# An encoder layer on one core: attention's scores and value products in three passes of rounded halves and rests, in place of full fp32 matmuls

## The chip, the core and the metric

The kernel runs on one core of a Trainium2 chip. The metric is the device time of one execution in microseconds (us); of several runs, the median.

## What is computed

One layer of a bidirectional encoder over 512 tokens of width 2048. The part that the change touches is attention with 8 query heads, 2 key and value heads and head width 128:

```python
q = rms_norm(q.reshape(B, S, ATT_HEADS, HEAD_DIM), q_norm_w)
k = rms_norm(k.reshape(B, S, ATT_KV_HEADS, HEAD_DIM), k_norm_w)
q = apply_axial_rope(q, cos, sin) * (HEAD_DIM ** -0.5)
k = apply_axial_rope(k, cos, sin)
...
s = jnp.einsum('bqhgd,bkhd->bhgqk', q_blk, k).astype(jnp.float32)
p = jax.nn.softmax(s, axis=-1).astype(v.dtype)
return jnp.einsum('bhgqk,bkhd->bqhgd', p, v)
```

Around it stand a conditioning product (`mod`), an input projection `h @ w_in` whose other columns feed a gated linear recurrence (HGRN2, 8 heads), an output projection, and a feed-forward part (up projection, convolution of width 3, GeGLU, down projection). All is float32.

## The kernel before

Five instruction streams (TensorE, VectorE, ScalarE, GpSimd and SyncE with the DMA queue) are written out by hand and tied by semaphores. An engine executes its own stream in order, so what stands behind a waiting instruction waits too.

The large projections don't use fp32 matmuls. Each operand is kept as a half `hi` rounded to the type fp32r and a rest `lo` = value - `hi`. `three_passes` (L1285 to L1288) adds three fp32r matmuls of 128x128 by 128x512 into one PSUM bank: hi by lo, hi by hi, lo by hi. `split_hi` (ScalarE, L437) and `split_lo` (VectorE, L818) make the two parts of each block of weights. Attention's own products are single calls on fp32 tiles instead.

TensorE's stream through the attention stage is a chain of query tiles (`q_tile`). A tile has 16 steps `s`. Each step is one `three_passes` of the input projection (`project_step`), and the attention of the head before hangs between the steps. For head h, whose query tile was projected just before:

- After step 2, `rope_mm` (L1319, L1320): two fp32 matmuls, for the sum of squares and the rotated copy of the queries. Keys use it as well, as r = 0 and 1 (`kv_side`, within the first query tile); head h has r = h + 2.
- On ScalarE, `rope_front` copies the projected tile out of PSUM (L482, L483), which also frees what the PE needs for the next `rope_mm`, and it waits for `rope_done` of the r before. `rope_rs` (L487, L489) makes 1/rms with a logarithm and an exponential.
- On VectorE, `rope_back` (L893 to L900): four tensor operations of 128x512, the last of which writes the tile `QT` (or `KTT` for keys) and signals `rope_done`.
- After steps 7 to 10, `scores` (L1336): one fp32 matmul for each of four blocks of 128 queries, into a bank each. The first waits for `rope_done`.
- VectorE at steps 8 to 12: `att_max` (L904) for each block, and `att_scale` (L909, L911) one step behind; between them ScalarE's `att_exp` (L496).
- After steps 12 to 15, `turn_probs` (L1346): four transposes of a block of probabilities into bank 6 or 7 in turn. Block qt waits until the copy of block qt - 2 has left the bank.
- ScalarE at step 12 `vsa_copy` (L513, the values into `VSA`) and at steps 13 to 15 and step 1 of the next tile `pt_copy` (L503, bank into `PT`).
- After step 4 of the tile after next, `att_values` (L1355): four fp32 matmuls into bank 2; then ScalarE's `att_store` (L518).

VectorE makes its two `split_lo` of the next tile at steps 5 and 7, between `rope_back` and `att_max`. Head 7 has no query tile behind it; its attention hangs in the first recurrence head (`hg_head`), whose steps `g` carry on VectorE a `split_lo` at g = 4 and 12 and a `chunk_row` (L1033, L1036) at g = 6, 10 and 14.

```python
def turn_probs(h, qt):
    n = h * TT + qt
    pe.wait_ge(prob_ready, n + 1)
...
        pe.wait_ge(pt_ready, n - 1)
```

Of the kernel before, what the change touches and what calls it, by code (L numbers as in the profile page):

```python
# [27 lines left out]
F32 = mybir.dt.float32  # L28
# [79 lines left out]
def hybrid_encoder_layer(nc, x, c, w_ada, b_ada, norm_mix_pre, norm_mix_post, w_in, q_norm, k_norm,  # L108
# [44 lines left out]
    KTT = at("KTT", [P, KV_HEADS, S], F32, OV)  # L153
    V2 = at("V2", [P, KV_HEADS, S], F32, OV + 4 * KB)
    VSA = at("VSA", [P, TT, P], F32, OV + 8 * KB)
# [4 lines left out]
    QT = at("QT", [P, S], F32, OV + 20 * KB)  # L160
    PM = [at(f"PM{n}", [P, S], F32, OV + o * KB) for n, o in enumerate((22, 24, 18, 38))]
    PT = at("PT", [P, TT, S], F32, OV + 26 * KB)
# [42 lines left out]
    with ExitStack() as ctx:  # L205
# [26 lines left out]
        prob_turned, pt_ready, att_pv, att_out = sem("prob_turned"), sem("pt_ready"), sem("att_pv"), sem("att_out")  # L232

# [189 lines left out]
        def _(act):  # L423
# [75 lines left out]
            def pt_copy(h, qt):  # L499
                act.wait_ge(prob_turned, h * TT + qt + 1)  # L500
                if qt == 0 and not (isinstance(h, int) and h == 0):
                    act.wait_ge(att_pv, h)
                act.activation(PT[:, :, qt * P:(qt + 1) * P],  # L503
                               PB[6 + qt % 2][:, :].rearrange("p (k q) -> p k q", q=P), ACT.Copy).then_inc(pt_ready, 1)

            def vsa_copy(h, group):

                if isinstance(h, int) and h == 0:
                    act.wait_ge(v_ready, KV_HEADS)
                else:  # L510
                    act.wait_ge(att_pv, h)
                src = V2[:, group, :] if isinstance(group, int) else V2[:, bass.ds(group, 1), :]
                act.activation(VSA[:, :, :].rearrange("p a b -> p (a b)"), src, ACT.Copy).then_inc(vsa_ready, 1)  # L513
# [293 lines left out]
        def _(dve):  # L807
# [81 lines left out]
            def rope_back(r, dst):  # L889
# [6 lines left out]
                dve.wait_ge(rope_t, r * 2 + 1)  # L896
                dve.tensor_tensor(SQA[:, :], T1[:, :], SQA[:, :], ALU.add).then_inc(rope_t, 1)
                dve.wait_ge(rope_t, r * 2 + 2)
                dve.wait_ge(rope_rstd, r + 1)
                dve.tensor_tensor(dst, SQA[:, :], RSA[:, :], ALU.mult).then_inc(rope_done, 1)  # L900
# [12 lines left out]
            def att_side(h, s):  # L913
                if s == 2:
                    rope_back(h + KV_HEADS, QT[:, :])
# [5 lines left out]
            def q_tile(i, e, first):  # L921
                h = i * 2 + e
                for s in range(16):
                    if first and e == 0 and s in (3, 9):
                        rope_back(s // 9, KTT[:, s // 9, :])
                    if not (first and e == 0):
                        att_side(h - 1, s)
# [3 lines left out]
            q_tile(0, 0, True)  # L931
            q_tile(0, 1, True)
            with dve.Fori(1, ATT_HEADS // 2) as i:
                q_tile(i, 0, False)
                q_tile(i, 1, False)
# [109 lines left out]
            def hg_head(h, i, e, first):  # L1045
                for g in range(STEPS):
                    bank = ((g // 16) + e + 1) % 2
                    if first and e == 0:
                        if g < 16:
                            att_side(ATT_HEADS - 1, g)  # L1050
# [185 lines left out]
        def _(pe):  # L1236
# [93 lines left out]
            def scores(h, group, qt):  # L1330
# [4 lines left out]
                rhs = KTT[:, group, :] if isinstance(group, int) else KTT[:, bass.ds(group, 1), :]  # L1335
                pe.matmul(PB[SCORE_BANKS[qt]][:, :], QT[:, qt * P:(qt + 1) * P], rhs, start=True, stop=True).then_inc(score_done, 1)  # L1336

            def turn_probs(h, qt):
# [4 lines left out]
                else:  # L1343
                    pe.wait_ge(pt_ready, n - 1)
# [356 lines left out]
```

## Time and profile before

| what | value |
|---|---|
| median of 3 runs | 2675.48 us (2674.86 to 2677.21) |
| profiled execution: span of the trace | 2672.3 us |
| TensorE matmul busy | 2580.3 us, 97% |
| VectorE busy | 1293.3 us, 48% |
| ScalarE busy | 833.6 us, 31% |
| TensorE in the chain that ended last | 92% |
| attention stage, from the first key rope to the last value product | about 204 to 398 us of the span |

The span is that of the profiled execution, from its first to its last instruction; the run's own time holds some 3 us around it. A matmul's length in the trace holds the time that its data take through the array, so that matmuls overlap in it: for their pace one reads start to start. A weight load (PEld) runs beside the matmul before.

### The profile page before, as it was taken

What the parts mean: (1) busy time and instruction counts of PE and PEld (TensorE: products, weight loads), DVE (VectorE), ACT (ScalarE), POOL (GpSimd) and SP (SyncE); (2) the same over time, 40 slices, a digit from 0 to 9 for tenths busy, and PEclk for the clock granted to TensorE, in tenths of its full rate; (3) what the DMA queues carried; (4) which work ended last, traced back from release to release, by engine and by line L of the source; (5) the groups of instructions that cost most, each with busy time, mean ns of one, the idle gap of its engine ahead of it and who ended that gap; (6) DMA issues with size and microseconds to landing.
All of it is one profiled execution on the core that took longest, in us unless ns stands there. A gap on an engine that the chain in (4) does not pass through costs nothing.

```text
span 2672.3 us, 32532 instructions
## 1 busy us (share of the span) xinstructions
PE 2580.3 (97%) x11944; PEld 2077.9 (78%) x11944; DVE 1293.3 (48%) x1538; ACT 833.6 (31%) x1112; POOL 6.5 (0%) x16
## 2 busy tenths in 40 slices
PE   5889999999999998989999999999999999999998
PEld 3446668888888877877888888888888878888887
DVE  4774456667766655345333333333333333334334
ACT  5116652222222232234222222222222222323222
POOL 0000000000000000000000000000000000000000
PEclk9889999999999999999999999999999999999999
DMA  7872136555655542423333333333333333222422
GB/s 229 229 201 65 47 104 219 166 181 181 193 169 174 169 129 68 177 96 110 102 100 96 94 94 94 94 97 102 100 94 94 94 110 100 96 94 98 162 94 110
DMA packets 396373, 335.78 MB, mean 126 GB/s; under 512 B 9670, under 2 KB 354720, under 8 KB 394016
## 3 DMA queue, kind: packets, MB, share of 16 engines
q1 hardware_dynamic: 394816, 324.54, 39.9%
q0 software_dynamic: 1504, 10.50, 1.0%
q8 instruction: 37, 0.61, 0.1%
q14 instruction: 16, 0.13, 0.0%
HBM read 326.60 MB, written 8.40 MB: 125 GB/s over the span
## 4 chain that ended last, share of the span: by engine, by line
PE 92%; DMA 3%; DVE 3%; ACT 2%; SPq 1%; issue 1%; DVEq 0%; ACTq 0%
PE bank L1286 27%; PE bank L1288 26%; PE bank L1287 26%; DMA AS_raw<-in_w_ada_dram 3%; PE bank L1456 2%; PE bank L1454 2%; PE bank L1250 1%; PE bank L1489 1%; PE bank L1355 1%; PE bank L1336 1%; PE bank L1476 1%; PE bank L1519 1%; PE bank L1346 0%; DVE ACC L856 0%; SPq L316 0%
## 5 line engine op out<-in xcount | busy, mean ns | idle before, releaser
L1286 PE MATMUL bank<-H_lo,W_hi 128*128 128x512 f32 x2240 | 918.5, 410 | 1.7 <-ACT QW L483 1.4
L1288 PE MATMUL bank<-H_hi,W_lo 128*128 128x512 f32 x2240 | 875.3, 391 | 0.0
L1287 PE MATMUL bank<-H_hi,W_hi 128*128 128x512 f32 x2240 | 874.4, 390 | 0.0
L818 DVE TENSOR_TENSOR W_lo<-W_raw,W_hi 128x1024 fp32r<-128x1024 f32 x400 | 481.2, 1222 | 200.8 <-ACT W_hi L437 189.7
L1286 PEld LDWEIGHTS bank<-H_lo,W_hi 128*128 128x128 f32 x2240 | 421.8, 188 | 109.4 <-issue 30.0
L1287 PEld LDWEIGHTS bank<-H_hi,W_hi 128*128 128x128 f32 x2240 | 422.1, 188 | 94.8 <-issue 15.3
L1288 PEld LDWEIGHTS bank<-H_hi,W_lo 128*128 128x128 f32 x2240 | 421.3, 188 | 89.8
L437 ACT ACTIVATE W_hi<-W_raw 128x1024 fp32r<-128x1024 f32 x400 | 410.6, 1049 | 169.7 <-DMA W_raw<-in_w_in_dram 73.9
L1286 PE MATMUL bank<-W_lo,GS_hi 128*128 128x512 f32 x704 | 275.4, 391 | 4.7 <-DVE GS_lo L1190 4.7
L1287 PE MATMUL bank<-W_hi,GS_hi 128*128 128x512 f32 x704 | 275.1, 391 | 0.0
L1288 PE MATMUL bank<-W_hi,GS_lo 128*128 128x512 f32 x704 | 275.1, 391 | 0.0
L1190 DVE TENSOR_TENSOR GS_lo<-G,GS_hi 128x512 fp32r<-128x512 f32 x88 | 60.7, 692 | 266.7 <-ACT GS_hi L771 266.7
L1036 DVE SCALAR_TENSOR_TENSOR AB_acc<-AB_raw,SM,AB_acc 128x1024 f32<-128x1024 f32 x120 | 153.8, 1281 | 25.9 <-DMA AB_raw<-in_w_ada_dram 24.8
L1153 DVE SCALAR_TENSOR_TENSOR CA<-bank,VEC,CA 128x511 f32<-128x511 f32 x44 | 33.0, 750 | 264.4 <-ACT CA L734 264.4
L1286 PEld LDWEIGHTS bank<-W_lo,GS_hi 128*128 128x128 f32 x704 | 132.8, 189 | 32.9 <-issue 5.1
L1287 PEld LDWEIGHTS bank<-W_hi,GS_hi 128*128 128x128 f32 x704 | 132.8, 189 | 27.5
L1288 PEld LDWEIGHTS bank<-W_hi,GS_lo 128*128 128x128 f32 x704 | 132.7, 189 | 27.6
L771 ACT ACTIVATE GS_hi<-G 128x512 fp32r (+1 forms) x88 | 55.3, 631 | 303.2 <-PE bank L1288 300.8
L734 ACT ACTIVATE CA<-bank,VEC 128x512 f32<-128x512 f32 x44 | 34.3, 779 | 356.6 <-PE bank L1288 356.6
L1153 DVE SCALAR_TENSOR_TENSOR CB<-bank,VEC,CB 128x511 f32<-128x511 f32 x44 | 33.0, 750 | 231.6 <-ACT CB L734 231.6
L734 ACT ACTIVATE CB<-bank,VEC 128x512 f32<-128x512 f32 x44 | 34.3, 779 | 254.8 <-PE bank L1288 254.8
L1286 PE MATMUL bank<-W_lo,H_hi 128*128 128x512 f32 x256 | 102.9, 402 | 7.4 <-DVE H_lo L1073 3.8
(185 smaller groups left out, 2077.9 us busy)
## 6 DMA issues: line engine op xcount, KB each, us to landing
W_raw<-in_w_up_dram SPq DMA_DIRECT2D x176, 512.0 KB, 4.5
AB_raw<-in_w_ada_dram SPq DMA_DIRECT2D x128, 512.0 KB, 4.5
W_raw<-in_w_in_dram SPq DMA_DIRECT2D x104, 512.0 KB, 4.0
W_raw<-in_w_down_dram SPq DMA_DIRECT2D x88, 512.0 KB, 3.5
AS_raw<-in_w_ada_dram SPq DMA_DIRECT2D x32, 1024.0 KB, 8.9
W_raw<-in_w_out_dram SPq DMA_DIRECT2D x32, 512.0 KB, 3.7
XT<-in_x_dram SPq DMA_DIRECT2D x4, 1024.0 KB, 8.0
XR<-in_x_dram POOLq DMA_DIRECT2D x4, 1024.0 KB, 12.6
```

The lines of the kernel that those rows point to most:

```text
L437: act.activation(W_hi[:, k % SLOTS, :], W_raw[:, k % RAW, :], ACT.Copy).then_inc(hi_ready, 1)
L734: act.activation(dst, PB[2 * e + half][:, :], ACT.Identity, bias=col(VEC, jj + V_CONVB), scale=col(VEC, jj + V_CONVW[1])).then_inc((ca_rea ...
L771: act.activation(GS_hi[:, k % SLOTS, :], src, ACT.Copy).then_inc(gs_hi, 1)
L818: dve.tensor_tensor(W_lo[:, k % SLOTS, :], W_raw[:, k % RAW, :], W_hi[:, k % SLOTS, :].bitcast(F32), ALU.subtract).then_inc(lo_ready, 1)
L1036: ins = dve.scalar_tensor_tensor(AB_acc[:, :], AB_raw[:, kt % 2, :], col(SM, CS + kt), AB_acc[:, :], ALU.mult, ALU.add)
L1153: dve.scalar_tensor_tensor(buf[:, e, 1:S], bank[:, 0:S - 1], col(VEC, jj + V_CONVW[0]), buf[:, e, 1:S], ALU.mult, ALU.add).then_inc(conv_l, 1)
L1190: dve.tensor_tensor(GS_lo[:, k, :], src, GS_hi[:, k, :].bitcast(F32), ALU.subtract).then_inc(gs_lo, 1)
L1286: pe.matmul(acc, st_hi, mv_lo, start=start, stop=False)
L1287: pe.matmul(acc, st_hi, mv_hi, start=False, stop=False)
L1288: return pe.matmul(acc, st_lo, mv_hi, start=False, stop=stop)
L1454: pe.matmul(halves(bank[:, t])[:, :, 1, :], YY[:, 0, t], halves(XX[:, 0, t])[:, :, 1, :], start=True, stop=True)
L1456: ins = pe.matmul(halves(bank[:, t])[:, :, 0, :], XX[:, 1, t], halves(YY[:, 1, t])[:, :, 0, :], start=True, stop=True)
```

## The change

Scores and value products go through `three_passes`. So every operand of theirs gets a rounded half and a rest.

- `KTT`, `QT`, `PT`, `VSA` become `KT_hi`, `QT_hi`, `PT_hi`, `VSA_hi` of type fp32r, and four tiles `_lo` are added where the recurrence's outputs are kept later.
- `rope_back` has two more instructions for each of its 10 calls, a cast to `hi` and a subtraction for `lo`, each behind a semaphore of the one before. `rope_done` comes after the last.
- VectorE gets `vsa_lower` (one for each head, at step 13) and `pt_lower` (four for each head, at steps 13 to 15 and step 1 of the next tile), which reads the transposed block in PSUM and subtracts `PT_hi`.
- `turn_probs` and `att_values` wait for `pt_low` and `vsa_low`, the subtractions, where they waited for ScalarE's copies.

```diff
-                dve.tensor_tensor(dst, SQA[:, :], RSA[:, :], ALU.mult).then_inc(rope_done, 1)
+                dve.tensor_tensor(T1[:, :], SQA[:, :], RSA[:, :], ALU.mult).then_inc(rope_t, 1)
+                dve.wait_ge(rope_t, r * 3 + 3)
+                dve.tensor_copy(hi, T1[:, :]).then_inc(rope_hi, 1)
+                dve.wait_ge(rope_hi, r + 1)
+                dve.tensor_tensor(lo, T1[:, :], hi.bitcast(F32), ALU.subtract).then_inc(rope_done, 1)
...
+            def vsa_lower(h, group):
+                dve.wait_ge(vsa_ready, h + 1)
+                src = V2[:, group, :] if isinstance(group, int) else V2[:, bass.ds(group, 1), :]
+                dve.tensor_tensor(VSA_lo[:, :, :].rearrange("p a b -> p (a b)"), src,
+                                  VSA_hi[:, :, :].rearrange("p a b -> p (a b)").bitcast(F32), ALU.subtract).then_inc(vsa_low, 1)
+
+            def pt_lower(h, qt):
+                dve.wait_ge(pt_ready, h * TT + qt + 1)
+                q = slice(qt * P, (qt + 1) * P)
+                dve.tensor_tensor(PT_lo[:, :, q], PB[6 + qt % 2][:, :].rearrange("p (k q) -> p k q", q=P),
+                                  PT_hi[:, :, q].bitcast(F32), ALU.subtract).then_inc(pt_low, 1)
...
+                if s == 13:
+                    vsa_lower(h, group)
+                if s >= 13:
+                    pt_lower(h, s - 13)
+
+            def att_tail(h, s):
+                if s == 1:
+                    pt_lower(h, TT - 1)
...
-                rhs = KTT[:, group, :] if isinstance(group, int) else KTT[:, bass.ds(group, 1), :]
-                pe.matmul(PB[SCORE_BANKS[qt]][:, :], QT[:, qt * P:(qt + 1) * P], rhs, start=True, stop=True).then_inc(score_done, 1)
+                keys = [t[:, group, :] if isinstance(group, int) else t[:, bass.ds(group, 1), :] for t in (KT_hi, KT_lo)]
+                q = slice(qt * P, (qt + 1) * P)
+                three_passes(PB[SCORE_BANKS[qt]][:, :], QT_hi[:, q], QT_lo[:, q], *keys, True, True).then_inc(score_done, 1)
...
-                    pe.wait_ge(pt_ready, n - 1)
+                    pe.wait_ge(pt_low, n - 1)
...
-                pe.wait_ge(pt_ready, h * TT + TT)
-                pe.wait_ge(vsa_ready, h + 1)
+                pe.wait_ge(pt_low, h * TT + TT)
+                pe.wait_ge(vsa_low, h + 1)
                 for k in range(TT):
-                    ins = pe.matmul(PB[2][:, :], VSA[:, k, :], PT[:, k, :], start=(k == 0), stop=(k == TT - 1))
+                    ins = three_passes(PB[2][:, :], VSA_hi[:, k, :], VSA_lo[:, k, :], PT_hi[:, k, :], PT_lo[:, k, :],
+                                       k == 0, k == TT - 1)
```

Two places of the order show it. In the changed kernel the lines of `three_passes` are L1320 to L1322 and the rope's are L898 to L909.

TensorE, steps 8 and 9 of a query tile with the scores between them, before:

```order
L1336 MATMUL bank<-KTT,QT 128x512
L1294 REGISTER_ALU
L1286 MATMUL bank<-H_lo,W_hi 128x512 [waits lo_ready]
L1287 MATMUL bank<-H_hi,W_hi 128x512
L1288 MATMUL bank<-H_hi,W_lo 128x512
L1336 MATMUL bank<-KTT,QT 128x512
```

The same place now:

```order
L1320 MATMUL bank<-KT_lo,QT_hi 128x512
L1321 REGISTER_ALU
L1321 MATMUL bank<-KT_hi,QT_hi 128x512
L1322 MATMUL bank<-KT_hi,QT_lo 128x512
L1328 REGISTER_ALU
L1320 MATMUL bank<-H_lo,W_hi 128x512 [waits lo_ready]
L1321 MATMUL bank<-H_hi,W_hi 128x512
L1322 MATMUL bank<-H_hi,W_lo 128x512
```

Each fp32 score has become three passes; the steps between them are as they were.

VectorE, from the last scale of a head (the tile `PM_87`) to the rope of the next, before:

```order
L911 TENSOR_SCALAR PM_87<-PM_87,SM 128x512 [waits prob_rcp]
L890 REGISTER_ALU
L893 TENSOR_TENSOR T_82<-QW,COS 128x512 [waits rope_in]
L895 TENSOR_TENSOR SQA<-bank,SIN 128x512 [waits rope_psum]
L896 ISA
L897 TENSOR_TENSOR SQA<-T_82,SQA 128x512 [waits rope_t]
L898 REGISTER_ALU
L900 TENSOR_TENSOR QT<-SQA,RSA 128x512 [waits rope_rstd,rope_t]
```

Now, from behind that scale and a wait for `vsa_ready`:

```order
L925 TENSOR_TENSOR VSA_lo<-V_77,VSA_hi 128x512
L931 TENSOR_TENSOR PT_lo<-bank,PT_hi 128x4x128 [waits pt_ready] x4
L895 REGISTER_ALU
L898 TENSOR_TENSOR T_82<-QW,COS 128x512 [waits rope_in]
L900 TENSOR_TENSOR SQA<-bank,SIN 128x512 [waits rope_psum]
L901 ISA
L902 TENSOR_TENSOR SQA<-T_82,SQA 128x512 [waits rope_t]
L903 REGISTER_ALU
L905 TENSOR_TENSOR T_82<-SQA,RSA 128x512 [waits rope_rstd,rope_t]
L906 REGISTER_ALU
L907 CAST QT_hi<-T_82 128x512 [waits rope_t]
L909 TENSOR_TENSOR QT_lo<-T_82,QT_hi 128x512 [waits rope_hi]
```

Five subtractions stand where VectorE had nothing, and two instructions stand behind the rope's product.

## Rows read from the trace of the kernel before

**Rows 1.** The page: busy time of the engines; the chain by line.

```profile
PE 2580.3 (97%) x11944; PEld 2077.9 (78%) x11944; DVE 1293.3 (48%) x1538; ACT 833.6 (31%) x1112; POOL 6.5 (0%) x16
...
PE bank L1286 27%; PE bank L1288 26%; PE bank L1287 26%; DMA AS_raw<-in_w_ada_dram 3%; PE bank L1456 2%; PE bank L1454 2%; PE bank L1250 1%; PE bank L1489 1%; PE bank L1355 1%; PE bank L1336 1%; PE bank L1476 1%; PE bank L1519 1%; PE bank L1346 0%; DVE ACC L856 0%; SPq L316 0%
```

**Rows 2.** TensorE's waits from 200 to 400 us: us in total, times, longest.

```profile
PE bank L1286 <- ACT QW L483: 1.4, 1, 1.4
PE bank L1346 <- ACT PT L503: 0.8, 1, 0.8
PE bank L1319 <- ACT QW L483: 0.6, 1, 0.6
```

**Rows 3.** Groups by line and form: busy us, mean ns of one, idle before.

```profile
L1336 PE MATMUL bank<-KTT,QT 128*128 x48 | 24.5, 592 | 0.0
...
L895 DVE TENSOR_TENSOR SQA<-bank,SIN 128x512 f32<-128x512 f32 x10 | 6.9, 691 | 21.3 <-PE bank L1320 21.3
...
L1143 DVE CAST H_hi<-HT 128x512 fp32r<-128x512 f32 x8 | 3.4, 421 | 0.0
```

**Rows 4.** Timeline of TensorE, head 3: start us, us, instruction.

```profile
291.67 0.39 PE L1287 MATMUL bank<-H_hi,W_hi 128*128 128x512 f32 x1
...
293.05 0.39 PE L1287 MATMUL bank<-H_hi,W_hi 128*128 128x512 f32 x1
...
294.60 0.40 PE L1287 MATMUL bank<-H_hi,W_hi 128*128 128x512 f32 x1
...
299.27 0.40 PE L1287 MATMUL bank<-H_hi,W_hi 128*128 128x512 f32 x1
...
302.67 0.60 PE L1346 MATMUL bank<-ident,PM 128*128 128x128 f32 x4
```

**Rows 5.** Timeline of TensorE, steps of the first query tile.

```profile
220.35 0.39 PE L1286 MATMUL bank<-H_lo,W_hi 128*128 128x512 f32 x1
...
223.07 0.39 PE L1286 MATMUL bank<-H_lo,W_hi 128*128 128x512 f32 x1
```

**Rows 6.** Timelines of VectorE, then ScalarE, head 3.

```profile
289.54 0.69 DVE L900 TENSOR_TENSOR QT<-SQA,RSA 128x512 f32<-128x512 f32 x1 [1.31 <-ACT RSA L489]
...
299.23 0.69 DVE L904 TENSOR_REDUCE SM<-bank 128x1 f32<-128x512 f32 x1 [0.27 <-PE bank L1336]
...
300.77 0.16 DVE L909 RECIPROCAL SM<-SM 128x1 f32<-128x1 f32 x1 [0.26 <-ACT PM L496]
...
299.96 0.69 ACT L496 ACTIVATE PM<-bank,SM 128x512 f32<-128x512 f32 x1 [0.70 <-DVE SM L904]
...
301.16 0.59 ACT L503 ACTIVATE PT<-bank 128x512 f32<-128x512 f32 x1
```

**Rows 7.** Timelines of VectorE, then ScalarE, around the ropes of the keys.

```profile
212.19 0.69 DVE L900 TENSOR_TENSOR KTT<-SQA,RSA 128x512 f32<-128x512 f32 x1 [1.32 <-ACT RSA L489]
...
213.41 0.59 ACT L482 ACTIVATE SQA<-bank 128x512 f32<-128x512 f32 x1
```

**Rows 8.** Timeline of TensorE before and at head 0's first score.

```profile
228.69 0.39 PE L1288 MATMUL bank<-H_hi,W_lo 128*128 128x512 f32 x1
229.15 1.13 PE L1336 MATMUL bank<-KTT,QT 128*128 128x512 f32 x2
```

**Rows 9.** Timelines of VectorE, ScalarE and TensorE, head 7.

```profile
384.56 1.28 DVE L1036 SCALAR_TENSOR_TENSOR AB_acc<-AB_raw,SM,AB_acc 128x1024 f32<-128x1024 f32 x1
...
388.23 1.23 DVE L818 TENSOR_TENSOR W_lo<-W_raw,W_hi 128x1024 fp32r<-128x1024 f32 x1 [0.26 <-ACT W_hi L437]
...
386.48 0.69 ACT L496 ACTIVATE PM<-bank,SM 128x512 f32<-128x512 f32 x1 [1.61 <-DVE SM L904]
...
389.35 0.63 PE L1346 MATMUL bank<-ident,PM 128*128 128x128 f32 x4 [0.83 <-ACT PT L503]
```

**Rows 10.** TensorE's timeline at the down projection; window with granted clock (seventh value).

```profile
2181.39 0.76 PE L1286 MATMUL bank<-W_lo,GS_hi 128*128 128x512 f32 x1 [4.73 <-DVE GS_lo L1190]
...
2182.00:2186.00 4.00, 4.00 (x11) 3.12 (x10) 3.45 (x4) 2.02 (x3) 0.00 (x0) 0.50 0.21 61
```

More of the change, by code:

```diff
@@ L151, in hybrid_encoder_layer @@
     OV = WK + 24 * KB
-    KTT = at("KTT", [P, KV_HEADS, S], F32, OV)
+    KT_hi = at("KT_hi", [P, KV_HEADS, S], F32R, OV)
     V2 = at("V2", [P, KV_HEADS, S], F32, OV + 4 * KB)
-    VSA = at("VSA", [P, TT, P], F32, OV + 8 * KB)
+    VSA_hi = at("VSA_hi", [P, TT, P], F32R, OV + 8 * KB)
     QW = at("QW", [P, S], F32, OV + 10 * KB)
@@ L159, in hybrid_encoder_layer @@
     T1 = at("T1", [P, S], F32, OV + 16 * KB)
-    QT = at("QT", [P, S], F32, OV + 20 * KB)
+    QT_hi = at("QT_hi", [P, S], F32R, OV + 20 * KB)
     PM = [at(f"PM{n}", [P, S], F32, OV + o * KB) for n, o in enumerate((22, 24, 18, 38))]
-    PT = at("PT", [P, TT, S], F32, OV + 26 * KB)
+    PT_hi = at("PT_hi", [P, TT, S], F32R, OV + 26 * KB)
+    PT_lo = at("PT_lo", [P, TT, S], F32R, MXB + 16 * KB)
+    KT_lo = at("KT_lo", [P, KV_HEADS, S], F32R, MXB + 24 * KB)
+    VSA_lo = at("VSA_lo", [P, TT, P], F32R, MXB + 28 * KB)
+    QT_lo = at("QT_lo", [P, S], F32R, MXB + 30 * KB)
     COS = at("COS", [P, S], F32, OV + 34 * KB)
@@ L232, in hybrid_encoder_layer @@
         prob_turned, pt_ready, att_pv, att_out = sem("prob_turned"), sem("pt_ready"), sem("att_pv"), sem("att_out")
+        rope_hi, pt_low, vsa_low = sem("rope_hi"), sem("pt_low"), sem("vsa_low")
         sig_ready, stage_ready, vt_ready, vs_turned, vs_ready = (
@@ L502, in pt_copy @@
                     act.wait_ge(att_pv, h)
-                act.activation(PT[:, :, qt * P:(qt + 1) * P],
+                act.activation(PT_hi[:, :, qt * P:(qt + 1) * P],
                                PB[6 + qt % 2][:, :].rearrange("p (k q) -> p k q", q=P), ACT.Copy).then_inc(pt_ready, 1)
@@ L886, in _, with rope_back @@
             split_lo(0, 4, 9)
-            def rope_back(r, dst):
+            def rope_back(r, hi, lo):
                 dve.wait_ge(rope_in, r + 1)
@@ L919, in att_side, with q_tile @@
                     att_scale(h, s - 9)
-            def q_tile(i, e, first):
+                if s == 13:
[5 more added lines that the diff above has]
+                    pt_lower(h, TT - 1)
+            def q_tile(i, e, first, group):
                 h = i * 2 + e
@@ L924, in q_tile @@
                     if first and e == 0 and s in (3, 9):
-                        rope_back(s // 9, KTT[:, s // 9, :])
+                        rope_back(s // 9, KT_hi[:, s // 9, :], KT_lo[:, s // 9, :])
                     if not (first and e == 0):
-                        att_side(h - 1, s)
+                        att_side(h - 1, group, s)
+                    if not first:
+                        att_tail(h - 2, s)
                     if s - 1 in SPLIT_STEPS:
                         split_lo(i, 4, 2 * ATT_PROLOGUE + 2 * e + 2 + SPLIT_STEPS.index(s - 1))
-            q_tile(0, 0, True)
-            q_tile(0, 1, True)
+            q_tile(0, 0, True, 0)
+            q_tile(0, 1, True, 0)
             with dve.Fori(1, ATT_HEADS // 2) as i:
-                q_tile(i, 0, False)
-                q_tile(i, 1, False)
+                q_tile(i, 0, False, i // 3)
+                q_tile(i, 1, False, i // 2)
             def stage(h, j, bank):
@@ L1049, in hg_head @@
                         if g < 16:
-                            att_side(ATT_HEADS - 1, g)
+                            att_side(ATT_HEADS - 1, KV_HEADS - 1, g)
+                            att_tail(ATT_HEADS - 2, g)
+                        elif g < 32:
+                            att_tail(ATT_HEADS - 1, g - 16)
                     else:
```

10 lines of the change are left out of this document (5 added, 5 removed).

## Prediction

> **What bounds the kernel now.** I read the page first. TensorE's matmuls are busy 97% of the span, and the chain that ended last lies almost wholly on them, mostly on the three lines of `three_passes` [rows 1]. So a saved TensorE microsecond counts, and a new TensorE wait costs in full. The second view is TensorE's waits in the attention stage: three in 200 us, 2.8 us in all [rows 2]. Each belongs to the structure that the change touches: the first copy of a projected tile (1.4 us), the second key rope (0.6), and head 7's third block of transposes (0.8). Everywhere else VectorE and ScalarE keep ahead of TensorE. The question is whether they still do with more work on VectorE and less on TensorE.
>
> **What the fp32 matmuls cost.** In head 3 two plain steps start 1.38 us apart (291.67 to 293.05), 0.69 us for a step of three passes. Three steps with a score between them take 294.60 to 299.27, 1.557 us each [rows 4]. So a score costs 1.557 - 0.69 = 0.867 us on the path. The trace has 48 records at 592 ns and 16 of the other form for the 32 scores, two for each call [rows 3]. The 32 calls of the value product have the same operand sizes, and I give them the same price. That makes 64 fp32 calls. Three passes cost 0.69 us, as in the plain step: 0.867 - 0.69 = 0.177, times 64 is **-11.3 us**.
>
> The score's 0.867 us is four times 0.217 us, but a pass of fp32r takes 0.230. The Trainium skill ("FP8 and Floating Point Precision", TensorE Precision Notes) says that true FP32 takes four passes through the array, which the 0.867 fits. The Trainium skill ("TensorE: Matmul & The Clock Gate", section "Wait — 56ns, not 53.3ns?") gives 215.7 ns from start to start for 512 columns at the full clock; the fp32 calls agree with it, the fp32r passes of this kernel do not. By that figure of the Trainium skill the gross gain would be 64 x 0.216 = 13.8 us, an estimate; I go by the rows.
>
> A smaller gain: away from fp32 instructions a step is shorter. In the first query tile four steps take 223.07 - 220.35 = 2.72 us, 0.68 each [rows 5]. This pace comes some four steps behind the last fp32 instruction. Now 18 triples stand in a head between the rope and the first transposes (10 steps, 4 scores, 4 products), with fp32 work no longer between them; 14 of them at 0.01 less, 8 heads: -1.1 us. Since VectorE's chain below doesn't shorten with them, I take **-0.7**.
>
> **The new work on VectorE.** A subtraction of 128x512 with a PSUM source takes 0.69 us (L895), a cast of that size 0.42 (L1143) [rows 3]. Where the next doesn't wait, starts are 0.08 closer. The end of a rope moves by 0.42 + 0.69 and two semaphores of 0.04: +1.15 us. Each head also gets five subtractions, 5 x 0.69 = 3.5 us. VectorE is half idle, so only the places where TensorE waits for it count. I go through them in the order of the program.
>
> 1. **Ropes of the keys.** The product of key head 0 ends at 212.19 + 0.69 = 212.88, and ScalarE starts the next `rope_front` at 213.41 [rows 7]: 0.53 of slack, of which ScalarE needs about 0.1 for the semaphore. Of the 1.15 us some 0.7 arrive at the second key rope, whose matmul waits already (0.6 us) [rows 2]. **+0.7.** The rope behind it loses nothing more: it waits for the projection, which has moved too.
> 2. **Head 0's first score.** The pass before starts at 228.69, so TensorE was free at 228.92, and the score starts at 229.15, right behind the rope's end [rows 8]. There is no slack here, since head 0 has no value product in front of its scores: **+1.15.** In heads 1 to 6 the product ends at 289.54 + 0.69 = 290.23 [rows 6] and the first score comes two steps behind the step whose second pass starts at 291.67 [rows 4], at about 293.5: 3.3 us of slack. It shrinks by 1.15 and by the 4 x 0.177 = 0.7 that the value product gives, and 1.4 us is left. Nothing there.
> 3. **The third block of transposes, heads 1 to 6.** `turn_probs` 2 now waits for the subtraction of block 0. Count from the start of the last score, which lies 0.867 and a pass before 299.27, at 298.18 [rows 4]. The last maximum starts at 299.23, 1.05 later; now 0.88. Its exponential starts 0.73 after it, the copy of block 0 1.20 after that (and runs 0.59), the reciprocal of block 3 0.81 after the exponential [rows 6]; the scale is issued 0.2 later and takes VectorE another 0.4. So VectorE is free for `vsa_lower` at 0.88 + 0.73 + 1.41 = 3.02, for `pt_lower` 0 at 3.63, and this ends at 4.32, plus 0.06. TensorE starts the third block at 302.67, 4.49 after the last score [rows 4]; with the score 0.177 shorter it wants to at 4.31. It is a near tie: 0.05 to 0.15 us, six heads, **+0.7.** Between scores VectorE has 1.28 us of work where TensorE will bring a score each 1.38: it holds.
> 4. **The same in head 0.** There both `split_lo` stand between the rope and the first maximum, so VectorE comes late to the scores and runs at its own pace of 1.28 a block from there. The rope moves all of it by 1.15 us; TensorE starts its first score later by the same, but its four scores then take 4 x 0.177 = 0.7 less, and VectorE's chain doesn't: **+0.7.**
> 5. **Head 7.** In its steps VectorE also has a `chunk_row` of 1.28 us before the last maximum, and a `split_lo` whose half is ready only 1.75 us after the last exponential (386.48 to 388.23); TensorE waits 0.83 us there today [rows 9]. With the value product and the scores shorter, TensorE comes to its third block at about 387.0 (start of the first score 378.5, three scores of 1.38, then 4.31). VectorE: maximum of block 2 at 382.1, scale of block 1 until 383.3, `chunk_row` until 384.5, then the last maximum; exponential at 385.3; `split_lo` from 387.0 to 388.15; `vsa_lower`, `pt_lower` 0 until 389.5. The wait is 2.5 in place of 0.8: **+1.7.**
>
> The new subtractions at step 1 of the next tile end before the rope's matmuls; the value products at step 4 stand 2 us behind them. The chunk rows of head 7 slip by some 4 us, with 7 us to the sum that needs them.
>
> **Sum.** -11.3 - 0.7 + 0.7 + 1.15 + 0.7 + 0.7 + 1.7 = -7.05; I take -6.8, since each of the waits was rounded down. Of the profiled span that is 2672.3 - 6.8 = 2665.5, and of the median of the runs, which stands 3.2 above the span, **2668.7 us**, 0.25% less. A measurement of this kernel can tell about 0.2%, 5.4 us, from no change, so the forecast lies only just outside.
>
> **Rivals.**
> - *The wait of head 7 lets the clock fall.* After 4.73 us without matmuls at the down projection the granted clock was 0.50 for the four microseconds behind it, the lower of the two levels, 1.2 GHz, which cost some 2.2 us [rows 10]. Behind head 7's 0.83 us nothing fell. A wait of 2.5 us lies between. Price: 2668.7 + 2.2 = 2670.9. The key rope's 1.4 us speaks against. Chance 0.07.
> - *The new passes run at the pace of fp32's own.* If 0.217 is the pace wherever both operands are small tiles of attention's, each of the 64 calls saves another 3 x 0.013 = 0.04 us: 2666.2. Against: the fp32r passes behind and before take 0.230. Behind it stands the second rule of the Trainium skill above, from "TensorE: Matmul & The Clock Gate". Chance 0.05.
> - *Semaphores come earlier than I count, and the blocks and the rope hide.* Then only the first 12 us stand: 2663.5. Head 0's missing slack speaks against. Chance 0.04.
> - *Part is given back.* The near tie of item 3 is one in six heads: if VectorE's instructions with register operations between them take 0.4 us more in the chain from the last exponential, that is +2.6, and any slip in the recurrence heads, where the loads follow VectorE's subtractions, adds to it: 2671.5 to 2675. Chance 0.13.
> - *Slower.* One mechanism: `pt_lower` 0 comes late in every head because it queues behind `vsa_lower` on an engine that executes in order. It decides from 0.85 us later than I count (6.8 / 8). If the pair took twice its time, 1.3 us more in 8 heads, the result is 2668.7 + 10.4 = 2679.1. Against: rows of the same form and size are steady at 0.69. Chance 0.04.
>
> **How the numbers follow.** The forecast itself has 0.67; its own spread (2667 to 2671) leaves 0.62 of that faster by over 0.2% and 0.05 within. With the second and third rival: faster 0.71. Within 0.2%: 0.05 + 0.07 + 0.13 = 0.25. Slower 0.04. The range goes from 2665.5 (the pace rival inside, all-hidden outside) to 2672.5 (the clock rival and the smaller part of what may be given back inside).
>
> **What would show it.** Steps with a score 1.38 us apart. TensorE's waits in the stage: about 1.4 us at the second key rope, 1.4 at head 0's first score, 0.7 at head 0's third block of transposes, 0.1 in heads 1 to 6, 2.5 in head 7; some 7.5 in all with the unchanged 1.4, where 2.8 stand now. The stretch from the first key rope to the last value product is 6.8 us shorter, and all that follows has its old length. Wrong would be: waits of 1 us in every head, a granted clock under 1.0 in the stage, or a later stage that grows by what this one saves.

## The result, and the profile after

The changed kernel takes 2682.64 us (median of 20 runs, 2677.97 to 2688.23), the kernel before, run beside it, 2675.78 us (20 runs). The ratio is 1.0028, 95% interval 1.0021 to 1.0035: slower by 0.28%, where 0.25% faster was forecast. The range ended at 2672.5 us.

The attention stage did get shorter. A later stage, in whose code nothing was changed, grew by twice as much. The table cuts both traces at the same events of TensorE, each at the weight load of the matmul named (spans of one profiled execution of each, us):

| stretch | before | after | difference |
|---|---|---|---|
| start to the first key rope's second matmul | 208.0 | 212.1 | +4.1 |
| to the recurrence's first diagonal product (attention stage) | 238.2 | 233.5 | -4.7 |
| to its last (heads of the recurrence) | 549.6 | 559.5 | +9.9 |
| to the output projection's transposes | 209.4 | 211.0 | +1.6 |
| to the first product with `GS_lo` (up projection) | 976.7 | 976.7 | 0 |
| to the end | 490.4 | 490.4 | 0 |

The +1.6 is a fall of the clock that comes and goes (below). Start to rope is no effect of the change: in the 13 profiles of this study it lies between 205.6 and 213.4, and neither with nor without the change is it steady. Without it the two traces differ by 6.8 us, and the medians by 6.9. Two of the signs that the prediction had set for its own failure are here: a later stage that grows, and a granted clock under 1.0 in the attention stage (the experiment with head 7, below).

The page of the changed kernel: TensorE's busy time is up by under 1 us [rows 1], so what is lost is waiting. The two last lines are queues that the first part of this document did not look at, on which the engines fetch their instructions. Columns: packets, MB, share of 16 DMA engines.

```profile
PE 2581.1 (96%) x12008; PEld 2094.6 (78%) x12008; DVE 1328.4 (50%) x1598; ACT 834.2 (31%) x1112; POOL 6.5 (0%) x16
...
q8 instruction: 55, 0.90, 0.1%
q14 instruction: 26, 0.21, 0.0%
```

The same lines of the kernel before:

```profile
q8 instruction: 37, 0.61, 0.1%
q14 instruction: 16, 0.13, 0.0%
```

TensorE's waits of the changed kernel in the attention stage, 200 to 450 us (total, times, longest):

```profile
PE bank L1381 <- DVE PT_lo L931: 2.8, 2, 2.5
PE bank L1353 <- ACT QW L488: 1.4, 1, 1.4
PE bank L1320 <- ACT QW L488: 1.4, 1, 1.4
PE bank L1320 <- DVE QT_lo L909: 1.3, 1, 1.3
```

These are the waits that the prediction lists: the second key rope 1.4, head 0's first score 1.3, head 7's third block 2.5. In the kernel before, the rows to compare are [rows 2].

Now TensorE's waits from 450 to 1010 us, in the heads of the recurrence:

```profile
PE bank L1477 <- DVE KD L995: 4.5, 2, 2.6
PE bank L1320 <- issue: 4.1, 3, 1.5
PE bank L1320 <- DVE GW L977: 1.5, 1, 1.5
```

The wait for `KD`, twice, is new, and "issue" is time in which the engine waited for nothing that the profile shows. The recurrence heads 2 to 7 are a loop of three passes with two heads each, on every engine that works on them. VectorE's timeline where it jumps back to the loop's start (start us, us, instruction, idle before and its releaser), first before:

```profile
671.00 0.17 DVE L1043 COPY MOD<-bank 128x8 f32 x1 [1.09 <-PE bank L1519]
674.49 0.75 DVE L946 SCALAR_TENSOR_TENSOR GW<-bank,VEC,SG 128x512 f32<-128x512 f32 x1 [3.33 <-ACT SG L592]
```

and after:

```profile
670.40 0.17 DVE L1074 COPY MOD<-bank 128x8 f32 x1 [0.89 <-PE bank L1555]
678.36 0.75 DVE L977 SCALAR_TENSOR_TENSOR GW<-bank,VEC,SG 128x512 f32<-128x512 f32 x1 [7.79 <-issue]
```

Before, VectorE stands 3.33 us for ScalarE's sigmoid, which is its ordinary slack. After, it stands 7.79 us for nothing that the profile shows. On TensorE the chain arrives as a hole:

```profile
679.62 0.39 PE L1322 MATMUL bank<-H_hi,W_lo 128*128 128x512 f32 x1
681.93 1.66 PE L1477 MATMUL bank<-QS,KD 128*128 128x128 f32 x8 [1.92 <-DVE KD L995]
```

Windows of the second and third pass of the loop, before and after, each from one jump back of TensorE to the next (window, length; busy us of PE, PEld, DVE, ACT, POOL with counts; granted clock; DMA share; GB/s):

```profile
669.50:824.40 154.90, 154.90 (x813) 129.93 (x814) 107.54 (x139) 41.93 (x50) 0.00 (x0) 1.00 0.56 176
824.40:979.40 155.00, 155.00 (x815) 130.01 (x814) 107.74 (x139) 41.94 (x50) 0.00 (x0) 1.00 0.56 176
```

```profile
668.90:829.20 160.30, 157.04 (x813) 130.97 (x814) 107.44 (x139) 41.95 (x50) 0.00 (x0) 0.99 0.56 171
829.20:990.10 160.90, 157.03 (x814) 131.10 (x814) 107.44 (x139) 41.96 (x50) 0.00 (x0) 0.99 0.55 171
...
682.40:685.80 3.40, 3.40 (x13) 2.91 (x12) 2.48 (x3) 0.00 (x0) 0.00 (x0) 0.50 0.40 113
```

A pass of 155.0 us takes 160.3 and 160.9, with the same work in it. Behind the hole the granted clock is 0.50 (1.2 GHz) from 682.4 to 685.8, and again at 842.8, which makes the hole dearer. The two passes lose 11.3 us together; 1.4 us of it come back at the loop's exit, where the clock was 0.50 for 6.8 us before and for 3.4 us after.

The trace's packets on q8 and q14 carry times. Before, TensorE's queue q8 fetches at 645.9 and then not again until 994.4: the loop is fetched once. After, it fetches at 668.2, 669.8, 676.3, 689.5 and so on through every pass, and q14 at 668.4, 672.9, 676.4, 678.9, then from 828.7 on again.

### The profile page after: what moved, and what is told of

Read it like the earlier page. It is cut to its first block, busy times and chain, and to the rows that moved or that the text cites. A ratio compares the mean times of both kernels' runs of the same rounds, so it can differ in the third digit from the quotient of the medians.

```text
span 2683.2 us, 32741 instructions
## 1 busy us (share of the span) xinstructions
PE 2581.1 (96%) x12008; PEld 2094.6 (78%) x12008; DVE 1328.4 (50%) x1598; ACT 834.2 (31%) x1112; POOL 6.5 (0%) x16
## 4 chain that ended last, share of the span: by engine, by line
PE 90%; DMA 3%; DVE 3%; ACT 1%; issue 1%; SPq 1%; DVEq 0%; ACTq 0%
PE bank L1320 27%; PE bank L1322 27%; PE bank L1321 27%; DMA AS_raw<-in_w_ada_dram 3%; PE bank L1492 2%; PE bank L1490 2%; PE bank L1284 2%; PE bank L1525 1%; PE bank L1381 1%; PE bank L1512 1%; PE bank L1555 1%; SPq L321 0%; PE bank L1477 0%; PE bank L1353 0%; DVE X L1265 0%
## 5 line engine op out<-in xcount | busy, mean ns | idle before, releaser
L1320 PE MATMUL bank<-H_lo,W_hi 128*128 128x512 f32 x2240 | 903.5, 403 | 4.3 <-issue 2.6
L1322 PE MATMUL bank<-H_hi,W_lo 128*128 128x512 f32 x2240 | 875.8, 391 | 0.0
L1320 PEld LDWEIGHTS bank<-H_lo,W_hi 128*128 128x128 f32 x2240 | 422.7, 189 | 105.7 <-issue 24.4
L1322 PEld LDWEIGHTS bank<-H_hi,W_lo 128*128 128x128 f32 x2240 | 421.9, 188 | 90.2
L1320 PE MATMUL bank<-W_lo,GS_hi 128*128 128x512 f32 x704 | 275.1, 391 | 4.7 <-DVE GS_lo L1224 4.7
L1322 PE MATMUL bank<-W_hi,GS_lo 128*128 128x512 f32 x704 | 274.8, 390 | 0.0
L1320 PEld LDWEIGHTS bank<-W_lo,GS_hi 128*128 128x128 f32 x704 | 132.8, 189 | 32.7 <-issue 5.1
L1322 PEld LDWEIGHTS bank<-W_hi,GS_lo 128*128 128x128 f32 x704 | 132.7, 188 | 27.8
L1284 PE MATMUL bank<-AS_raw,SM 128*1 128x128 f32 x512 | 80.6, 308 | 32.4 <-DMA AS_raw<-in_w_ada_dram 29.6
```

Source lines behind the costliest of these rows:

```text
L1284: ins = pe.matmul(PB[2 + kt % 2][0:1, 0:P], col(SM, CS + r), AS_raw[:, n % 3, r, :], start=(r == 0), stop=(r == KT - 1))
L1320: pe.matmul(acc, st_hi, mv_lo, start=start, stop=False)
L1322: return pe.matmul(acc, st_lo, mv_hi, start=False, stop=stop)
```

## The theory, and how the place of a loop is counted

Theory P: the change makes the programs of VectorE and TensorE longer ahead of the recurrence's loop. The loop's own instructions are unchanged, but they lie elsewhere over the pieces in which instructions are fetched, and there the loop is no longer kept between passes. The rivals: noise and attention's new waits (N), a clock that falls for its own reasons (W), and longer code as such (T).

The place is counted in the trace: all records of an engine in order, waits, branches and TensorE's weight loads included, a loop's passes counted once. VectorE's loop has 265 instructions and begins at 409 before and 446 after; TensorE's has 1702 and begins at 3787 and 3853. ScalarE's and SyncE's counts are unchanged. A packet on q8 is 16 KB and one on q14 8 KB. The Trainium skill ("Runtime: NRT & Kernel Launch", Instruction fetch mechanics) counts 16 KiB as 256 instructions, so a piece is taken as 256 instructions for TensorE and 128 for VectorE. The traces bear this out where the places of the packets are counted, below.

The padding is work that no one reads, placed where the engine is idle: VectorE from 2 to 11 us, TensorE from 11 to 25 us. A memset is one instruction; a matmul of one fp32 element is four in the trace, two weight loads and two matmuls.

```diff
             dve.memset(col(SM, EPSC), EPS)
+            for _pad in range(16):
+                dve.memset(PROD[:, 0, _pad:_pad + 1], 0.0)
...
             ins.then_inc(vec_turned, 1)
+            for _pad in range(40):
+                pe.matmul(PB[7][0:1, 0:1], ones[0:1, 0:1], ones[0:1, 0:1], start=True, stop=True)
             pe.wait_ge(c_ready, 1)
```

All versions in one table, in the order of the text (ratio to the kernel before, with interval; second and third pass of the loop in us):

| version | VectorE's loop at | TensorE's at | q14 | q8 | passes | ratio |
|---|---|---|---|---|---|---|
| before | 409 | 3787 | 16 | 37 | 154.9, 155.0 | 1 |
| after | 446 | 3853 | 26 | 55 | 160.3, 160.9 | 1.0028 (1.0021 to 1.0035) |
| after, VectorE +16 | 462 | 3853 | 17 | 55 | 156.4, 156.1 | 0.9989 (0.9980 to 0.9998) |
| after, TensorE +160 | 446 | 4013 | 26 | 38 | 160.2, 160.2 | 1.0030 (1.0020 to 1.0041) |
| after, both | 462 | 4013 | 16 | 38 | 154.9, 154.9 | 0.9983 (0.9974 to 0.9992) |
| before, VectorE +37, TensorE +64 | 446 | 3851 | 26 | 55 | 159.5, 160.2 | 1.0040 (1.0025 to 1.0055) |
| after, VectorE +4 | 450 | 3853 | 16 | 55 | 156.4, 156.3 | 0.9979 (0.9969 to 0.9988) |
| after, VectorE +124 | 570 | 3853 | 27 | 55 | 157.8, 160.4 | 1.0005 (0.9995 to 1.0015) |
| both, head 7 in another order | 462 | 4013 | 16 | 38 | 154.9, 154.9 | 0.9962 (0.9948 to 0.9975) |
| scores alone, TensorE +160 | 423 | 3981 | 16 | 56 | 161.0, 162.6 | 1.0037 (1.0023 to 1.0051) |
| values alone, TensorE +160 | 432 | 3979 | 16 | 56 | 160.8, 161.3 | 1.0047 (1.0033 to 1.0060) |
| scores alone, TensorE +200 | 423 | 4023 | 16 | 38 | 154.9, 154.9 | 1.0000 (0.9990 to 1.0010) |
| before, TensorE +192 | 409 | 3979 | 16 | 56 | 160.8, 160.1 | 1.0039 (1.0026 to 1.0052) |

## Experiments: padding alone

**The changed kernel, 16 memsets more on VectorE** (the first part of the diff above).

> The changed kernel with 16 tiny memsets more on VectorE at 2 us, where it idles until 11 us. Theory P (position in the program): the trace of the changed kernel has 18 instruction packets more on q8 (TensorE's pieces) and 10 more on q14 than before, because the change lengthens both programs ahead of the recurrence's loop and so shifts how the loop lies over the pieces that are fetched; by it 16 instructions more on VectorE put VectorE's loop (265 instructions) back over two fetch points in place of three: q14 falls from 26 packets to about 17, q8 stays near 55, VectorE's stands of 4 us behind its loop branches go, and the time falls by 2 to 8 us, to about 2677. Rival N (noise and the new waits of the attention stage): nothing moves beyond 1 us. Rival T (VectorE's code is only longer, and more of it is fetched): q14 stays at 26 or more.

Measured: 2672.87 us against 2675.79, q14 at 17, q8 still at 55, passes of 156.4 and 156.1. Sixteen instructions of 0.06 us make the kernel some 10 us faster than without them.

**40 matmuls of one element more on TensorE** (the second part).

> The changed kernel with 40 matmuls of one element (4 instructions each) more on TensorE at 11 us, where it idles until 25 us for a DMA. Theory P: TensorE's recurrence loop (1702 instructions) lies over six fetch points again in place of seven: q8 falls from 55 packets to about 38, q14 stays at 26; the stands of VectorE remain, so the time falls by 1 to 5 us. Rival N: within 1 us of the changed kernel. Rival V (VectorE's fetches alone cost the time): q8 falls but the time does not.

Measured: 2683.45 us, q8 back at 38, and no time gained. Rival V is right for this place: with VectorE late, TensorE's refetch adds nothing to the time. The passes are 160.2 and 160.2 us without it and 160.3 and 160.9 with it.

**Both.**

> The changed kernel with both paddings. Theory P: both queues back at about 37 and 16 packets; the recurrence stage loses its 9.9 us, and the kernel comes to about 2672, which is 3 to 6 us under the kernel before (the attention stage's 4.7 us saving remains). Rival N: stays at about 2682. Rival W (the slower recurrence comes from the clock, which falls four times there after the new data placement or heat): stays at 2680 to 2683 with the clock still falling to 0.5 in it.

Measured: 2669.93 us, ratio 0.9983, which is 4.5 us under the kernel before (2.1 to 7.0). Both passes are 154.9 us, and the attention stage is still 233.5. So the three passes of attention are worth some 5 us by themselves. Rival N falls. So does W as a cause: no fall of the clock lies in the loop any more.

**The kernel before with 37 and 64 instructions of padding** (both parts of the diff, 37 memsets and 16 matmuls, nothing of the change).

> The kernel before, with nothing of the change, but 37 tiny memsets more on VectorE at 2 us and 16 matmuls of one element (64 instructions) on TensorE at 11 us, so that both programs are shifted as the change shifts them. Theory P: q8 rises from 37 to about 55 packets and q14 from 16 to about 26, and it is 8 to 11 us slower than the kernel before, about 2685. Rival N or W (the loss belongs to the three passes): within 1 us of the kernel before.

Measured: 2685.49 us, 26 and 55 packets, passes of 159.5 and 160.2. The loss comes without attention's change. Its page:

```profile
q8 instruction: 55, 0.90, 0.1%
q14 instruction: 26, 0.21, 0.0%
```

and its waits on TensorE from 450 to 1010 us are those of the changed kernel under other line numbers:

```profile
PE bank L1445 <- DVE KD L966: 4.4, 2, 2.5
PE bank L1290 <- issue: 4.2, 3, 1.5
PE bank L1290 <- DVE GW L948: 1.5, 1, 1.5
```

## Experiments: where the edge lies

**Four memsets in place of 16.**

> The changed kernel with 4 tiny memsets more on VectorE at 2 us. In the runs so far VectorE's recurrence loop of 265 instructions was fetched once where it began at instruction 409 or 462 of VectorE's program, and in every iteration where it began at 446. Theory P1: a piece of 128 instructions is fetched when VectorE comes to the middle of the piece ahead (instructions 448, 576, 704), and a loop that passes three such points in an iteration evicts its own start; then 4 instructions (start 450) are enough: q14 16 or 17 packets, about 2673. Rival P2 (the distance matters, some 10 or more instructions): q14 26 packets, about 2682.

Measured: 2669.05 us, q14 at 16. VectorE's timeline behind the jump has its old shape again:

```profile
666.28 0.17 DVE L1076 COPY MOD<-bank 128x8 f32 x1 [1.09 <-PE bank L1557]
669.79 0.75 DVE L979 SCALAR_TENSOR_TENSOR GW<-bank,VEC,SG 128x512 f32<-128x512 f32 x1 [3.34 <-ACT SG L597]
```

**124 memsets.**

> The changed kernel with 124 tiny memsets more on VectorE at 2 us, which end before it has work at 11 us. VectorE's loop then begins at instruction 570. Theory P1: 570 lies to the points 576 and 704 as 446 did to 448 and 576, so the loop passes three points again: q14 26 packets or more, and 2680 to 2684 in spite of the padding. Rival P3 (any padding helps, by moving the program's or the data's place in memory): q14 near 17 and about 2673.

Measured: 2679.69 us, q14 at 27, passes of 157.8 and 160.4. The time lies about 10 us above the version with 4. So padding as such does not help, and 4 instructions are enough from 446. The loop is fetched again at 570 as at 446, but it costs less there: 1.0005 (0.9995 to 1.0015) against 1.0028 (1.0021 to 1.0035), intervals that don't meet. Why is open: in the traces the heads of the recurrence differ by 1.6 us only. P1 holds for VectorE: with fetch points, the places at which a further piece is asked for, 128 apart (one of them between 446 and 449), the loop is kept where two lie in it (409, 423, 432, 450, 462), and fetched again where three do (446, 570). The median is 0.3 us under the expected 2680 to 2684, in a round where the kernel before took 2676.65, and the profiled execution, at 2683.63, was the slowest of its 10 runs.

**Scores alone, and values alone, in three passes.** The first keeps `PT` and `VSA` in fp32 and drops `vsa_lower` and `pt_lower`; the second keeps `QT` and `KTT` in fp32 and drops the two instructions in `rope_back`. Both have 40 matmuls of padding.

```diff
-                    ins = three_passes(PB[2][:, :], VSA_hi[:, k, :], VSA_lo[:, k, :], PT_hi[:, k, :], PT_lo[:, k, :],
-                                       k == 0, k == TT - 1)
+                    ins = pe.matmul(PB[2][:, :], VSA_hi[:, k, :], PT_hi[:, k, :], start=(k == 0), stop=(k == TT - 1))
```

```diff
-                three_passes(PB[SCORE_BANKS[qt]][:, :], QT_hi[:, q], QT_lo[:, q], *keys, True, True).then_inc(score_done, 1)
+                pe.matmul(PB[SCORE_BANKS[qt]][:, :], QT_hi[:, q], keys, start=True, stop=True).then_inc(score_done, 1)
```

> Scores alone in three passes, the value products in fp32 as before; 40 matmuls of padding on TensorE, none on VectorE (its loop begins at about 424, which passes two points). By the terms of the prediction: 32 calls save 0.177 us each, -5.7, pace -0.35, key ropes +0.7, first score +1.15: stage -4.2, so 234.0 us from first rope to first diagonal, where before had 238.2; no wait for PT_lo and no fall of the clock. Rival (what the three-pass steps save is lost again to late operands): -2 or less. Time 2670 to 2672.

> Value products alone in three passes, the scores in fp32 as before; 40 matmuls of padding on TensorE, none on VectorE (its loop begins at about 432, which passes two points). By the terms of the prediction: 32 calls -5.7, pace -0.35, third block of transposes of heads 1 to 6 +0.7, of head 0 +0.7, head 7 +1.7, and the clock's fall behind it, which the changed kernel showed, +1.3: stage -1.6, so 236.6 us from first rope to first diagonal, where before had 238.2. Rival (heads 1 to 6 lose less than the sum has, as the changed kernel showed 0.24 each): within 0.7 us of it. The parts should add up: scores alone and values alone together save what both do (4.7). Time 2672 to 2674.

Measured: the times were wrong by far, 2687.32 and 2690.18 us, and the stages nearly right: 234.1 and 237.1 us from the first rope to the first diagonal (expected 234.0 and 236.6). Together they save 4.1 + 1.1 = 5.2 us of the stage, where both at once save 4.7 and the sum was expected to be the same. The loss lies in the loop's passes again, this time with q14 at 16 and q8 at 56. TensorE of the scores-only version stands in the pass by itself:

```profile
670.14 0.39 PE L1319 MATMUL bank<-H_hi,W_lo 128*128 128x512 f32 x1
673.45 0.70 PE L1317 MATMUL bank<-H_lo,W_hi 128*128 128x512 f32 x1 [2.92 <-issue]
```

So TensorE's loop at 3979 or 3981 is fetched again too, and it is not harmless there. My guess that TensorE's points lie at the middle of a piece was wrong: 3968 should have let 3979 through. From 3787 and 4013 (six points, kept) and 3851, 3853, 3979, 3981 (seven) the point lies between 3981 and 4012.

The trace of the kernel before had shown it. Counted the same way, 35 of its 37 packets on q8 start while TensorE is at 150 or more within a stretch of 256 instructions, the earliest at 150, 151 and 152; the other two start 25 and 29 us behind the end of an earlier and a later loop. So the points are 256 apart, and one lies at about 3990. VectorE's packets in the loop's first pass start at 450 and 578, 128 apart. In each later pass of the changed kernel they start at 575, at 706 and 710 (the loop ends at 710) and, behind the jump, at 446 and 449. The number of points in a loop follows from its length: 265 is 2 x 128 + 9, so by this count three points fall into VectorE's loop at only 9 of 128 places; 1702 is 6 x 256 + 166, so seven fall into TensorE's at 166 of 256.

Two kernels tried the point between 3981 and 4012:

> The version with the scores alone in three passes, with 50 in place of 40 padding matmuls on TensorE. With 40, TensorE's recurrence loop began at instruction 3981 and was fetched again in each iteration (56 packets on q8), which put its iterations at 161.0 and 162.6 us where the kernel before has 154.9; the guess that TensorE's fetch points lie at the middle of a piece of 256 was wrong by some instructions. Theory P (position alone): the loop begins at about 4021, and 4013 was good in two versions: q8 near 38 packets, iterations of 154.9 us, about 2670. Rival S (the scores-only version has a loss of its own in the recurrence): iterations stay above 158 us and the time above 2680.

> The kernel before with nothing but 48 matmuls of one element (192 instructions) of padding on TensorE, which runs them at 11 us while it has to wait until 25 us anyway. TensorE's recurrence loop then begins at about 3979, beside the two versions with 3979 and 3981 that were slow; VectorE is left as it was. Theory P: q8 about 56 packets, q14 16, iterations of 161 us, and 10 to 13 us slower than the kernel before, about 2688: TensorE's refetch alone costs as much as VectorE's when it falls at the loop's start. Rival Q (TensorE's refetch is harmless, as in the versions at 3853, where an iteration took 156.4 us): at most 3 us slower.

Measured: scores alone with its loop at 4023 has 38 packets and passes of 154.9 us, as expected. The kernel before with 192 idle instructions more on TensorE has 56 packets, passes of 160.8 and 160.1, and takes 2686.57 us: 0.39% slower, with nothing changed but the place. Its TensorE waits from 450 to 1010 us:

```profile
PE bank L1289 <- issue: 6.2, 2, 3.4
PE bank L1288 <- issue: 3.8, 3, 1.5
```

One miss stays: scores alone at 4023 has a trace 4.0 us shorter than before's from the first rope to the end (2460.4 against 2464.4), but its median, 2675.28 us, is level. Its profiled execution was the fastest of its 12. Without a profile of a median run it is not known where the others lose the 4 us.

## Experiment: head 7

On top of both paddings, in head 7 alone the copies and rests of the turned probabilities go first, and the weight split of that place and the values' split go behind them:

```diff
# ScalarE, hg_head
...
-                    if g % 8 == 3:
+                    late = first and e == 0
+                    if g % 8 == 3 and not (late and g == 11):
                         split_hi(i, 20, U_HG + 10 * e + LEAD + g // 8)
+                    if late and g == 14:
+                        split_hi(i, 20, U_HG + 10 * e + LEAD + 1)
...
# VectorE, att_side
+                last = isinstance(h, int) and h == ATT_HEADS - 1
-                if s == 13:
+                if s == 13 and not last:
                     vsa_lower(h, group)
                 if s >= 13:
                     pt_lower(h, s - 13)
+                if s == 14 and last:
+                    vsa_lower(h, group)
```

(`vsa_copy` likewise behind the second `pt_copy`; `split_lo` of g = 12 at g = 15.)

> The version with both paddings (2669.9), and in attention's last head the order on ScalarE and VectorE changed: the copies of the turned probabilities and their rests go ahead of the weight split that stood before them at step 11/12 (it moves to step 14/15), and the value block's split goes after the first of them. Theory: TensorE's wait of 2.49 us for PT_lo there becomes 0.3 to 0.6, and the clock no longer falls to 0.5 behind it (about 1.3 us), so the attention stage is 3.0 to 3.5 us shorter: 230.0 to 230.6 from first rope to first diagonal where it was 233.5, and the time is 2666 to 2667.5. Rival C (the clock falls anyway, from the shorter waits): 2 us shorter, about 2668. Rival L (the later weight split is waited for at step 24): a new wait on lo_ready and no gain.

Measured: 2664.92 us, ratio 0.9962 (0.9948 to 0.9975), the best version of the study; the stage is 229.8 us where it was 233.5 (expected 230.0 to 230.6, and 2666 to 2667.5 for the time). In the changed kernel the head's third block waited, and the clock fell behind it, as it did in all seven profiles in which this wait is 2.3 to 2.5 us long:

```profile
387.87 0.63 PE L1381 MATMUL bank<-ident,PM 128*128 128x128 f32 x4 [2.49 <-DVE PT_lo L931]
...
388.90:392.30 3.40, 3.40 (x12) 2.72 (x11) 1.91 (x3) 2.26 (x4) 0.00 (x0) 0.50 0.64 194
```

In the reordered version:

```profile
381.61 0.63 PE L1397 MATMUL bank<-ident,PM 128*128 128x128 f32 x4 [0.40 <-DVE PT_lo L939]
...
207.90:437.70 229.80, 225.99 (x1030) 178.49 (x1028) 160.25 (x249) 132.72 (x207) 0.00 (x0) 1.00 0.34 103
```

The wait went from 2.49 to 0.40 us, 2.1 less, and the granted clock stays at 1.00 through the stage. That leaves, as a difference, 1.6 us of the 3.7 for the fall of the clock. No new wait on the later weight split shows.

## Why the prediction was wrong

The sum was made for the attention stage, and there it mostly held; the step that failed stands in "What would show it": **"all that follows has its old length"**. The heads of the recurrence grew by 9.9 us. The prediction counted each added instruction by its time and its place in the queue, and not by what it does to the place of the code behind it. No rival had such a mechanism; "part is given back" named late loads in the recurrence heads and reached to 2675 only. The slower rival (0.04) named a mechanism in attention that did not come.

Where the trace of before could have told: q8 fetched nothing between 645.9 and 994.4, so the loop was kept, and a reader who asks what keeps it has the rival. The Trainium skill ("Runtime: NRT & Kernel Launch", Instruction fetch mechanics) gives 512 instructions of buffer for most engines and 2048 for TensorE, and says that a taken branch whose target is not held stalls for a fetch. The traces agree with the stall (7.79 us on VectorE, 2.92 us on TensorE). In pieces these figures are four for VectorE and eight for TensorE. The loops here were kept with two points and with six, two fewer each, and lost with three and with seven; that fits, and no other length of loop was tried. The same section calls the buffer two cache lines; a loop of 1702 instructions that passes without one fetch speaks against that for TensorE.

Point by point, by its own terms:

- **The fp32 calls, -11.3, and the pace, -0.7: right.** In steady heads rope follows rope at 21.42 us before and 20.18 after, 1.24 less. With the 0.24 of (3) added back that is 1.48, where the two terms make 12.0 / 8 = 1.50. Scores alone give 20.63, values alone 20.95: -0.79 and -0.47, together -1.26, as both do (-1.24). The score steps of the changed kernel are 1.36 us apart, where 1.38 was forecast:

```profile
297.03 0.39 PE L1321 MATMUL bank<-H_hi,W_hi 128*128 128x512 f32 x1
...
298.39 0.39 PE L1321 MATMUL bank<-H_hi,W_hi 128*128 128x512 f32 x1
...
299.75 0.39 PE L1321 MATMUL bank<-H_hi,W_hi 128*128 128x512 f32 x1
```

- **The rival of the pace came half true.** Behind the value product the passes start 0.227 us apart, neither 0.230 nor the 0.217 that would have been fp32's.
- **(1) Second key rope, +0.7: right.** The wait is 1.4 us, and the two key ropes are 7.96 us apart instead of 7.20.
- **(2) Head 0's first score, +1.15: right.** The wait is 1.26 us. Against the pass before, the score starts 1.41 late, where before it was 0.23 late: +1.18.
- **(3) Third block of heads 1 to 6, 0.05 to 0.15 each: half of what it is.** The pass before ends its turn at 304.28 + 0.23 = 304.51, and the block starts at 304.75: 0.24, six times, 0.7 us more than the +0.7. Values alone carry all of it, which is why they save 0.47 a head and not 0.7.

```profile
304.28 0.40 PE L1322 MATMUL bank<-H_hi,W_lo 128*128 128x512 f32 x1
304.75 0.63 PE L1381 MATMUL bank<-ident,PM 128*128 128x128 f32 x4
```

- **(4) Head 0's third block, +0.7: somewhat too much.** Counted as in (3), it starts at 244.21 where its turn was at 243.70: 0.51. The waits list 0.34.
- **(5) Head 7, 2.5 us: right to the digit; but behind it the clock fell,** the first rival, which had 0.07 and a price of 2.2. It cost 1.6. I had 0.83 and 1.4 us without a fall and 4.73 with one; 2.5 lay open, and 0.07 was too little for it.

The stage: -6.8 forecast, +1.6 for the clock, +0.7 for the third blocks, -0.2 for head 0 gives -4.7; measured -4.7. That it closes to the tenth is luck, since the forecast had rounded its own sum of -7.05. With VectorE's loop kept, the change alone stands at 0.9983 or 0.9979 of before (both paddings, 4 memsets), 2671.2 or 2670.2 us by these ratios: inside the range. The version with 16 memsets, whose VectorE loop is kept too, gives 0.9989 or 2672.8, just above it.

Still open: how the buffer works that a count of points decides it, and why TensorE's refetch costs 1.4 us a pass at 3853 and over 5 at 3979. The traces show where the difference arises: in both slow passes of the three versions at 3979 and 3981, TensorE stands idle for 2.6 to 3.4 us at instruction 4033 of its program, and at 3851 and 3853 it does not. Why there, no run shows.

## What to carry to other kernels

Before one prices an edit ahead of a loop, look whether the instruction queues rest while the loop runs: if they do, the loop is kept by its place, and a few instructions more on one engine can make every pass refetch it; count their packets before and after. When a stage whose code is unchanged gets slower, compare these counts first, then try padding with idle instructions: 4 were enough here for VectorE, while for TensorE the nearest good place that was tried lies 32 behind 3981. And an operand that becomes late by a few tenths in each head is cheap, while one long wait (2.3 to 2.5 us here) can also take the clock with it.

## What the runs showed of the hardware that I had not expected

- A loop's place in the program is worth 0.4% here: 2675.8 us with VectorE's loop at instruction 409, 2685.5 with the paddings; 4 instructions of 0.06 us take a changed kernel from 2682.6 to 2669.1.
- VectorE's loop of 265 and TensorE's of 1702 instructions are both kept for all passes when they lie well, on 16 and 37 packets for the whole program.
- The place where the next piece is asked for can be read from one trace by counting: about 150 within each 256 of TensorE's records here.
- Whether the clock falls behind a TensorE wait of some 2.2 us is not settled by the wait's length. Ahead of the output projection the kernel before waits 2.24 us, and its clock stays; the changed kernel waits the same 2.24 us, and the clock is 0.50 behind it. That is the +1.6 us of the first table, and the versions with both loops kept and with 4 memsets show the one and the other too (211.0 and 209.4 us). Of the 13 profiles, 8 have the fall there. Before, then after:

```profile
1058.85 0.50 PE L1286 MATMUL bank<-W_lo,H_hi 128*128 128x512 f32 x1 [2.24 <-DVE H_lo L1073]
1059.19 0.39 PE L1287 MATMUL bank<-W_hi,H_hi 128*128 128x512 f32 x1
```

```profile
1068.15 0.79 PE L1320 MATMUL bank<-W_lo,H_hi 128*128 128x512 f32 x1 [2.24 <-DVE H_lo L1107]
1068.74 0.63 PE L1321 MATMUL bank<-W_hi,H_hi 128*128 128x512 f32 x1
...
1068.10:1071.50 3.40, 3.35 (x8) 2.67 (x9) 0.00 (x0) 0.00 (x0) 0.00 (x0) 0.50 0.00 0
```
